# Forget attention: the causal mask added to the table on VectorE, and a pair's units from wide to narrow

## The chip, the cores and the metric

The kernel runs on one core of one Trainium2 chip. The metric is the device time of one execution in microseconds. TensorE multiplies, VectorE, ScalarE and GpSimd work on elements, SyncE and the other engines' queues start transfers. Each engine runs its own instruction stream in order, and waits on semaphores that the others raise.

## The reference, cut to what matters

The program is a whole two-block transformer on 512 tokens of width 1024. The change touches one operation of the second block, the causal softmax attention with forget gates: 8 heads of 64, blocks of 128 queries.

```python
def _forgetting_attention(q, k, v, log_f):
    c = jnp.cumsum(log_f, axis=1)
    ...
    def block(args):
        qi, ci, t0 = args
        s = jnp.einsum('bqhd,bkhd->bhqk', qi, k) * SCALE
        s = s + ci[..., None] - c_k[:, :, None, :]
        q_pos = t0 + jnp.arange(BLOCK_Q)
        s = jnp.where(k_pos[None, :] <= q_pos[:, None], s, NEG_INF_2)
        p = jax.nn.softmax(s, axis=-1)
        return jnp.einsum('bhqk,bkhd->bqhd', p.astype(v.dtype), v)
```

Ahead of it the same block computes a dilated attention of 8 more heads, which has a distance bias instead of the forget table. Behind it come the output projection, a router and the experts.

## The kernel before

Both attentions are computed by one loop over 32 units, listed in `TWO` (L1920): kind f (0 dilated, 1 forget), pair c of two heads, block i of 128 queries. A unit is as wide as its keys, (i + 1) x 128 columns (`width2`), so the four units of a pair go 128, 256, 384, 512. Units 0 to 15 are dilated, 16 to 31 forget. Every unit handles both heads of its pair (a = 0 and 1).

The steps of a unit:

- TensorE `scores(u)`: q times k of both heads into two PSUM banks, which alternate between units. In forget units two more products, `ident_b` times `causal_b` (L1989), add the mask (0 or -1e30, bf16) to the last 128 columns.
- VectorE `maxima(u)`: adds the table to the scores in PSUM and reduces the row's extreme (L2094), one instruction with an accumulator read for each head. For forget units the table is `CK[h]`, the head's forget sums, 512 columns wide in SBUF, the same for all four units of the pair.
- ScalarE `exps(u)`: exponentials and row sums (L2061).
- VectorE `normed(u)`: the reciprocal of the sums (L2099). It releases the scaling of the rows (L1960), which VectorE does for head 0 if the unit is wider than 256, and GpSimd for the rest, so for both heads of a narrow unit.
- TensorE `turned(u)`: transposes the rows in blocks (L1996). ScalarE copies head 0 out of PSUM (L2076), VectorE head 1 (L2119).
- TensorE `values(u)`: the rows times v (L2011), both heads, two products for each 128 keys.

The order is written out by hand. TensorE's iteration u is `scores(u + 2)`, `values(u - 1)`, `turned(u)`. VectorE's is `normed(u)`, `maxima(u + 2)`, after a pair's end `y2_low` (L2036, the low half of the finished output), and the copy of unit u. ScalarE's is `exps(u + 1)`, after a pair's end `y2_high` and `square2`, and its copy of unit u. GpSimd waits for each unit's reciprocal, scales, and after a pair adds up squares (L2132).

Three things are placed by unit number. `SUMS_AT = 22` puts the products that sum the dilated squares (L1965) ahead of the scores of unit 24, their result into `DIL_SUMS` (end of bank 0), its copy (L1970) ahead of that unit's maxima, and the split of a weight chunk of the output projection (L154, 128x2048, on VectorE) into iteration 24, behind the maxima of unit 26. `t_mx` is the semaphore that the maxima raise, 2 per unit, on which the exponentials wait, and SyncE too, for loading the second half of the forget table after unit 15.

Of the kernel before, what the change touches and what calls it, by code (L numbers as in the profile page):

```python
# [9 lines left out]
ALU = mybir.AluOpType  # L10
# [4 lines left out]
P = 128  # L15
D = 1024
T = 512
MT = T // P
# [44 lines left out]
def program(nc, a, out):  # L63
# [5 lines left out]
    with ctx:  # L69
# [37 lines left out]
        ident_b = sb("ident_b", [P, P], bf16)  # L107
# [1809 lines left out]
            src = bass.AP(bias_dram.tensor, half * 4 * TW, [[1, P], [TW, 4], [1, T]])  # L1917
            pool.dma_start(bias_raw[half], src).then_inc(b_ld, 16)

        TWO = [(f, c, i) for f in range(2) for c in range(4) for i in range(MT)]  # L1920
        NU2 = len(TWO)
        Y2_AT = {24: 0, 26: 1, 27: 2, 29: 3}
        tmin = sb("two_min", [P, 2, 2])
        tden = sb("two_den", [P, 4, 2])
        t_qk = Sig("attn_scores", NU2)
        t_mx = Sig("attn_max", 2 * NU2)
        t_ex = Sig("attn_exp", 2 * NU2)
        t_tr = Sig("attn_PT_mm", 2 * NU2)
        t_pa = Sig("attn_PT_head0", NU2)
# [14 lines left out]
        t_yl = Sig("attn_y_low", KT)  # L1944
        ACC = [JUNK[:, 0:512], WK[:, 0:512]]
        SQ = JUNK[:, 512:1024]
        SUMS_AT = 22

        def width2(u):
            return (TWO[u][2] + 1) * P  # L1950

        def normed2_at(u, a):
            wide = sum(width2(v) > 2 * P for v in range(u + 1))
# [15 lines left out]
            dve.wait_ge(t_ss, f + 1)  # L1969
            nc.vector.tensor_copy(stat[:, 8 + 4 * f:12 + 4 * f], o).then_inc(t_sc, 1)  # L1970

        DIL_SUMS, FOX_SUMS = PB[:, 0, 508:512], PB[:, 6, 0:4]

        def two_pe(pe):
            def scores(u):
                f, c, i = TWO[u]
                w = width2(u)
                q, k = ((qdT, kdT), (qfT, kfT))[f]
                if u >= 2:
                    pe.wait_ge(*t_ex.at(2 * u - 2))  # L1980
                if u == SUMS_AT + 2:
                    sums_pe(pe, 0, DIL_SUMS)
                for a in range(2):
                    h = slice(a * DH, (a + 1) * DH)
                    t = nc.tensor.matmul(PB[:, 2 * (u % 2) + a, 0:w], q[c][h, i * P:(i + 1) * P], k[c][h, 0:w],  # L1985
                                         start=True, stop=(f == 0))
                if f == 1:
                    for a in range(2):
                        t = nc.tensor.matmul(PB[:, 2 * (u % 2) + a, i * P:w], ident_b[:], causal_b[:], start=False, stop=True)  # L1989
                t.then_inc(t_qk.sem, 1)  # L1990

            def turned(u):
                for a in range(2):
                    pe.wait_ge(*normed2_at(u, a))
                    for b in range(width2(u) // P):
                        t = nc.tensor.transpose(PB[:, 4 + a, b * P:(b + 1) * P], PR2[:, u % 2, a, b * P:(b + 1) * P], ident[:])  # L1996
                    t.then_inc(t_tr.sem, 1)

            def values(u):
                f, c, i = TWO[u]  # L2000
                n = 4 * f + c
                if i == 0 and n >= 2:
                    pe.wait_ge(*t_yl.at(n - 1))
                    pe.wait_ge(*t_sq.at(n - 1))
                pe.wait_ge(*t_pa.at(u + 1))
                pe.wait_ge(*t_pb.at(u + 1))
                v0 = (VA_, VF_)[f] + c * P
                nb = width2(u) // P
                for b in range(nb):
                    for a in range(2):  # L2010
                        t = nc.tensor.matmul(PB[a * DH:(a + 1) * DH, 6 + n % 2, i * P:(i + 1) * P],  # L2011
                                             Z2[:, b, v0 + a * DH:v0 + (a + 1) * DH], PT2[u % 2][a][:, b, :],
                                             start=(b == 0), stop=(b == nb - 1))
                if i == MT - 1:
                    t.then_inc(t_out.sem, 1)

            p_2.wait_all(pe)
            turned_wait(pe, 4)
            scores(0)
            scores(1)  # L2020
            for u in range(NU2):
                if u + 2 < NU2:
                    scores(u + 2)
                if u >= 1:
                    values(u - 1)
                turned(u)
            values(NU2 - 1)
# [25 lines left out]

        def two_act(act):
            def exps(u):
                act.wait_ge(*t_mx.at(2 * u + 2))
                if u >= 2:
                    act.wait_ge(*t_tr.at(2 * u - 2))
                w = width2(u)
                for a in range(2):  # L2060
                    nc.scalar.activation(PR2[:, u % 2, a, 0:w], PB[:, 2 * (u % 2) + a, 0:w], ACT.Exp,  # L2061
                                         bias=tmin[:, u % 2, a:a + 1], scale=-1.0,
                                         accum_out=tden[:, u % 4, a:a + 1]).then_inc(t_ex.sem, 1)

            exps(0)
            for u in range(NU2):
# [8 lines left out]
                w = width2(u)  # L2075
# [7 lines left out]
        def two_dve(dve):  # L2083
            def maxima(u):
                f, c, i = TWO[u]
                w = width2(u)
                dve.wait_ge(*t_qk.at(u + 1))
                if u == SUMS_AT + 2:
                    sums_dve(dve, 0, DIL_SUMS)
                for a in range(2):  # L2090
                    h = 2 * c + a
                    table = CK[h][:, 0:w] if f else bias_raw[h // 4][:, h % 4, w - 1::-1]
                    s = PB[:, 2 * (u % 2) + a, 0:w]
                    nc.vector.tensor_tensor_reduce(s, s, table, -1.0, 3.0e38, ALU.add, ALU.min, tmin[:, u % 2, a:a + 1]  # L2094
                                                   ).then_inc(t_mx.sem, 1)
# [1104 lines left out]
```

## Time and profile before

| | |
|---|---|
| median of 3 runs | 1823.97 us (1823.07 to 1825.81) |
| the profiled execution's own time | 1824.19 us |
| its span in the profile | 1822.3 us |
| TensorE busy | 1769.0 us, 97% |
| VectorE busy | 866.0 us, 48% |
| ScalarE, GpSimd busy | 631.9 us (35%), 232.1 us (13%) |
| chain that ended last | TensorE 90%, VectorE 5%, ScalarE 3% |
| second attention stage | 1357 to 1440.6 us, forget half from about 1394 |

Times of the timeline count from the span's start. The profiled execution took 1.9 us more than its span. A row's duration is how long one instruction was in its engine; successive instructions of an engine overlap by some tens of ns up to 0.2 us, so the cost of one in a full stream is read from start to start.

### The profile page before, as it was taken

The numbers are of one execution on the slowest core, as the hardware profiler recorded it, in microseconds if no ns is written. First come the engines' busy times: TensorE is split into PE (matmuls) and PEld (weight loads), VectorE is DVE, ScalarE is ACT, GpSimd is POOL, SyncE is SP. The second block draws the span as 40 slices with busy tenths as digits, with TensorE's granted clock in tenths as the row PEclk, the third lists the DMA queues.
The fourth block names the chain that finished last, engine by engine and source line by source line (L and its number), as shares of the span: only waits on it lengthen the run. The fifth ranks groups of instructions, "written<-read, shape, count | busy, mean of one in ns | idle before, by whom it ended". The sixth has DMA issues, their size and how long they took to land.

```text
span 1822.3 us, 22718 instructions
## 1 busy us (share of the span) xinstructions
PE 1769.0 (97%) x9086; PEld 1301.2 (71%) x9086; DVE 866.0 (48%) x1684; ACT 631.9 (35%) x1257; POOL 232.1 (13%) x283
## 2 busy tenths in 40 slices
PE   7999999999999999999999999999999999999998
PEld 6778888888888887568888888888776674333333
DVE  4436544443366446745545443353447463333326
ACT  5236334332353224635443332253347430000002
POOL 4000000000000103310000000000004412333322
PEclk9999999999999998999999999999999999999999
DMA  7223333332232217403333322243230138999985
GB/s 242 92 71 85 101 92 92 92 106 102 93 121 93 70 63 228 117 24 93 93 92 98 107 96 93 93 138 93 71 115 24 56 156 350 369 377 395 392 348 184
DMA packets 182313, 260.41 MB, mean 143 GB/s; under 512 B 24785, under 2 KB 137633, under 8 KB 169936
## 3 DMA queue, kind: packets, MB, share of 16 engines
q1 hardware_dynamic: 159040, 204.66, 33.4%
q0 software_dynamic: 19152, 25.14, 4.5%
q10 hardware_dynamic: 4032, 29.36, 4.1%
q8 instruction: 63, 1.03, 0.2%
q14 instruction: 26, 0.21, 0.0%
HBM read 297.53 MB, written 27.82 MB: 179 GB/s over the span
## 4 chain that ended last, share of the span: by engine, by line
PE 90%; DVE 5%; ACT 3%; DMA 1%; issue 1%; POOL 0%; SPq 0%; DVEq 0%; ACTq 0%; POOLq 0%
PE PB L191 21%; PE PB L193 21%; PE PB L192 21%; PE PB L2762 9%; PE PB L2784 5%; PE PB L2751 1%; PE PB L1985 1%; PE PB L2011 1%; PE PB L1996 1%; PE PB L1589 1%; PE PB L1566 1%; DVE RING_R L154 1%; PE PB L322 1%; PE PB L1558 1%; ACT RING_R L169 1%
## 5 line engine op out<-in xcount | busy, mean ns | idle before, releaser
L191 PE MATMUL PB<-RING_R,OPS_R 128*128 128x512 f32 (+1 forms) x1056 | 414.5, 393 | 4.6 <-DVE RING_R L154 3.5
L193 PE MATMUL PB<-RING_R,OPS_R 128*128 128x512 f32 (+1 forms) x1056 | 409.0, 387 | 0.0
L192 PE MATMUL PB<-RING_R,OPS_R 128*128 128x512 f32 (+1 forms) x1056 | 408.8, 387 | 0.0
L171 DVE SCALAR_TENSOR_TENSOR RING_R<-RING,gains,RING_R 128x256 fp32r<-128x256 f32 (+2 forms) x456 | 219.4, 551 | 254.3 <-ACT RING_R L169 254.3
L191 PE MATMUL PB<-OPS_R,RING_R 128*128 128x512 f32 (+1 forms) x736 | 280.7, 381 | 0.0
L192 PE MATMUL PB<-OPS_R,RING_R 128*128 128x512 f32 (+1 forms) x736 | 279.5, 380 | 0.0
L193 PE MATMUL PB<-OPS_R,RING_R 128*128 128x512 f32 (+1 forms) x736 | 279.5, 380 | 0.0
L191 PEld LDWEIGHTS PB<-RING_R,OPS_R 128*128 128x128 f32 x1056 | 198.9, 188 | 48.0 <-DVE RING_R L154 4.7
L169 ACT ACTIVATE RING_R<-RING,gains 128x256 fp32r<-128x256 f32 (+2 forms) x456 | 209.9, 540 | 59.7 <-DMA RING<-in_w_in 48.1
L193 PEld LDWEIGHTS PB<-RING_R,OPS_R 128*128 128x128 f32 x1056 | 198.7, 188 | 40.5
L192 PEld LDWEIGHTS PB<-RING_R,OPS_R 128*128 128x128 f32 x1056 | 198.9, 188 | 38.7 <-issue 0.2
L154 DVE TENSOR_TENSOR RING_R<-RING,RING_R 128x2048 fp32r<-128x2048 f32 x40 | 91.6, 2293 | 185.8 <-ACT RING_R L151 185.7
L191 PEld LDWEIGHTS PB<-OPS_R,RING_R 128*128 128x128 f32 x736 | 138.4, 188 | 26.5 <-issue 0.5
L192 PEld LDWEIGHTS PB<-OPS_R,RING_R 128*128 128x128 f32 x736 | 138.4, 188 | 26.5 <-issue 0.5
L193 PEld LDWEIGHTS PB<-OPS_R,RING_R 128*128 128x128 f32 x736 | 138.4, 188 | 26.4
L151 ACT ACTIVATE RING_R<-RING 128x2048 fp32r<-128x2048 f32 x40 | 76.4, 1913 | 199.9 <-DMA RING<-in_ffn_w_down 137.0
L806 ACT ACTIVATE WK<-WK 128x512 f32<-128x512 f32 x44 | 27.8, 632 | 278.5 <-DVE WK L829 278.5
L2826 ACT ACTIVATE WK<-PB 128x256 f32<-128x256 f32 x24 | 9.2, 383 | 279.3 <-PE PB L2762 279.3
L2865 DVE TENSOR_TENSOR WK<-PB,WK 128x256 f32<-128x256 f32 x24 | 14.7, 614 | 142.1 <-ACT WK L2826 141.7
L399 ACT ACTIVATE Z<-PB,stat 128x512 f32<-128x512 f32 (+1 forms) x34 | 22.8, 674 | 113.8 <-PE PB L193 113.8
L829 DVE TENSOR_TENSOR WK<-PB,Y 128x512 f32<-128x512 f32 x44 | 30.4, 690 | 63.7 <-PE PB L193 63.2
L3011 POOL DMA_DIRECT2D GP<-in_od_cmp_v_w x1 | 1.2, 1173 | 460.6 <-DVE X L578 460.6
(395 smaller groups left out, 2061.4 us busy)
## 6 DMA issues: line engine op xcount, KB each, us to landing
RING<-in_ffn_w_gate SPq DMA_DIRECT2D x44, 512.0 KB, 4.0
RING<-in_ffn_w_up SPq DMA_DIRECT2D x44, 512.0 KB, 5.3
RING<-in_ffn_w_down SPq DMA_DIRECT2D x44, 512.0 KB, 4.0
RING<-in_w_expert_gate SPq DMA_DIRECT2D x16, 1024.0 KB
RING<-in_w_expert_up SPq DMA_DIRECT2D x16, 1024.0 KB
OPS<-in_w_expert_gate SPq DMA_DIRECT2D x16, 1024.0 KB
OPS<-in_w_expert_up SPq DMA_DIRECT2D x16, 1024.0 KB
Y<-in_w_expert_down ACTq DMA_DIRECT2D x14, 1024.0 KB
```

The lines of the kernel that those rows point to most:

```text
L151: nc.scalar.activation(RING_R[:, high], RING[:, raw], ACT.Copy).then_inc(s_whi, 1)
L154: nc.vector.tensor_tensor(RING_R[:, raw], RING[:, raw], RING_R[:, high].bitcast(fp32), ALU.subtract).then_inc(s_wlo, 1)
L169: t = nc.scalar.activation(high, raw, ACT.Copy, scale=g)
L171: t = nc.vector.scalar_tensor_tensor(by_k(RING_R, o)[:, :, k, :], raw, g, high.bitcast(fp32), ALU.mult, ALU.subtract)
L191: nc.tensor.matmul(o, x[0], w[0], start=start, stop=False)
L192: nc.tensor.matmul(o, x[0], w[1], start=False, stop=False)
L193: return nc.tensor.matmul(o, x[1], w[0], start=False, stop=stop)
L399: t = nc.scalar.activation(dst, src, func, scale=rstd) if self.norm.deferred else nc.scalar.activation(dst, src, func)
L806: nc.scalar.activation(SIL[:, k, :], SIL[:, k, :], ACT.Silu).then_inc(self.sl.sem, 1)
L829: nc.vector.tensor_tensor(SIL[:, k, :], PB[:, BANK[k], :], rows, ALU.mult).then_inc(self.gs.sem, 1)
L2762: t = nc.tensor.matmul(PB[h, 2 + s % 2, :], XgT[:, s % 2, k, h], moe_gu[g][:, b, :, k, :], start=(k == 0), stop=(k == KT - 1))
L2784: t = nc.tensor.matmul(PB[h, 6 + hf, :], HhT[:, s % 2, j, h], moe_d[s % 2][:, b, j, hf * 512:(hf + 1) * 512], start=(j == 0), stop=(j == 1))
```

## The change

TensorE's two mask products per forget unit go. In their place VectorE adds `causal_b` to the last 128 columns (`i * P` to `w`) of the head's table `CK[h]`, in place in SBUF, for both heads, before the maxima of the unit (L2095 of the new file), behind the wait for the unit's scores. Ahead of the additions it waits for its own maxima of the unit before, which read the same table; behind them it waits for the additions. Since a narrower unit does not read the columns that a wider one has masked, the forget units of a pair now run from 512 down to 128. The semaphore of the maxima counts four per forget unit. A pair's first and last unit are told by u % 4. `SUMS_AT` is 21, so that sums, their copy and the split stand one unit earlier, and `DIL_SUMS` lies in bank 2, whose unit (23) is 128 wide.

```diff
-        TWO = [(f, c, i) for f in range(2) for c in range(4) for i in range(MT)]
+        TWO = [(f, c, MT - 1 - i if f else i) for f in range(2) for c in range(4) for i in range(MT)]
...
-        t_mx = Sig("attn_max", 2 * NU2)
+        t_mx = Sig("attn_max", 3 * NU2)
...
-        SUMS_AT = 22
+        SUMS_AT = 21
...
+        def max_at(u, masked=0):
+            f = TWO[u][0]
+            return t_mx.at(2 * u + 2 * max(u - NU2 // 2, 0) + (masked or 2 + 2 * f))
...
-        DIL_SUMS, FOX_SUMS = PB[:, 0, 508:512], PB[:, 6, 0:4]
+        DIL_SUMS, FOX_SUMS = PB[:, 2, 508:512], PB[:, 6, 0:4]
...
-                                         start=True, stop=(f == 0))
-                if f == 1:
-                    for a in range(2):
-                        t = nc.tensor.matmul(PB[:, 2 * (u % 2) + a, i * P:w], ident_b[:], causal_b[:], start=False, stop=True)
+                                         start=True, stop=True)
...
-                if i == 0 and n >= 2:
+                if u % MT == 0 and n >= 2:
...
-                if i == MT - 1:
+                if u % MT == MT - 1:
...
-                act.wait_ge(*t_mx.at(2 * u + 2))
+                act.wait_ge(*max_at(u))
...
+                if f:
+                    dve.wait_ge(*max_at(u - 1))
+                    for a in range(2):
+                        last = CK[2 * c + a][:, i * P:w]
+                        nc.vector.tensor_tensor(last, last, causal_b[:], ALU.add).then_inc(t_mx.sem, 1)
+                    dve.wait_ge(*max_at(u, 2))
```

VectorE around a pair's end, before: from the copy of unit 17 to the first head of unit 20's maxima and on to the scaling of unit 19. COPY is L2119, TENSOR_SCALAR the scaling, ISA the maxima (PB is PSUM, Y holds the tables), SCALAR_TENSOR_TENSOR `y2_low`.

```order
L2119 COPY Z<-PB 128x256
L2099 RECIPROCAL two_den<-two_den 128x2
L1960 TENSOR_SCALAR ST<-ST,two_den,ones 128x384
L2094 ISA PB,two_min<-PB,Y 128x128
L2094 ISA two_min 128x1
L2094 ISA PB,two_min<-PB,Y 128x128
L2094 ISA two_min 128x1
L2036 SCALAR_TENSOR_TENSOR OPS_R<-PB,gains,OPS_R 128x512
L2119 COPY Z<-PB 128x384
L2099 RECIPROCAL two_den<-two_den 128x2
L1960 TENSOR_SCALAR ST<-ST,two_den,ones 128x512
```

The same place in the changed kernel, from the copy of unit 17 to the maxima of unit 20 and the reciprocal of unit 19:

```order
L2126 COPY Z<-PB 128x384
L2106 RECIPROCAL two_den<-two_den 128x2
L2095 TENSOR_TENSOR Y<-Y,causal_b 128x128 x2
L2101 ISA PB,two_min<-PB,Y 128x512
L2101 ISA two_min 128x1
L2101 ISA PB,two_min<-PB,Y 128x512
L2101 ISA two_min 128x1
L2037 SCALAR_TENSOR_TENSOR OPS_R<-PB,gains,OPS_R 128x512
L2126 COPY Z<-PB 128x256
L2106 RECIPROCAL two_den<-two_den 128x2
```

The two additions stand ahead of the maxima, the 512-wide maxima stand ahead of `y2_low` and of the copy of the 256-wide unit, and no scaling is VectorE's at a pair's end.

TensorE at the seam of the two attentions, before, from the scores of unit 16 (L1985), their masks (L1989), values (L2011) and turning (L1996) in turn:

```order
L1985 MATMUL PB<-Z 128x128 x2
L1989 MATMUL PB<-causal_b,ident_b 128x128 x2
L2011 MATMUL PB<-Z 64x128 x4
L1996 MATMUL PB<-ident,ST 128x128 x6
L1985 MATMUL PB<-Z 128x256 x2
L1989 MATMUL PB<-causal_b,ident_b 128x128 x2
L2011 MATMUL PB<-Z 64x128 x6
L1996 MATMUL PB<-ident,ST 128x128 x8
```

And in the changed kernel, from the scores of unit 16 on:

```order
L1989 MATMUL PB<-Z 128x512 x2
L2012 MATMUL PB<-Z 64x128 x4
L1997 MATMUL PB<-ident,ST 128x128 x6
L1989 MATMUL PB<-Z 128x384 x2
L2012 MATMUL PB<-Z 64x128 x6
L1997 MATMUL PB<-ident,ST 128x128 x8
L1989 MATMUL PB<-Z 128x256 x2
L2012 MATMUL PB<-Z 64x128 x8
```

The mask products are gone, and the wide scores come first, so that unit 16 is as wide as unit 15.

## Rows read from the trace of the kernel before

**Rows 1.** The page: engine, busy us (share of the span), instructions

```profile
PE 1769.0 (97%) x9086; PEld 1301.2 (71%) x9086; DVE 866.0 (48%) x1684; ACT 631.9 (35%) x1257; POOL 232.1 (13%) x283
```

**Rows 2.** Chain that ended last, forget half: start us, us, engine, tile, line

```profile
1394.52 0.81 PE PB L2011 x12
...
1404.30 0.81 PE PB L2011 x12
...
1408.59 1.06 PE PB L1985 x4
1409.65 0.22 PE PB L1989 x2
...
1410.23 0.59 PE PB L1996 x4
...
1414.49 0.81 PE PB L2011 x12
...
1427.11 0.81 PE PB L2011 x12
...
1440.64 0.43 PE PB L191
```

**Rows 3.** Timeline of VectorE, one pair: start us, us, line, operation, idle before

```profile
1401.39 0.42 DVE L2119 COPY Z<-PB 128x256 f32<-128x256 f32 x1
1401.72 0.16 DVE L2099 RECIPROCAL two_den<-two_den 128x2 f32<-128x2 f32 x1
1401.92 0.48 DVE L1960 TENSOR_SCALAR ST<-ST,two_den,ones 128x384 f32<-128x384 f32 x1
1402.31 0.29 DVE L2094 CUSTOM_DVE_ANT_0 PB<-PB,Y 128x128 f32<-128x128 f32 x1
...
1402.77 0.75 DVE L2036 SCALAR_TENSOR_TENSOR OPS_R<-PB,gains,OPS_R 128x512 fp32r<-128x512 f32 x1
1403.49 0.56 DVE L2119 COPY Z<-PB 128x384 f32<-128x384 f32 x1
1403.96 0.15 DVE L2099 RECIPROCAL two_den<-two_den 128x2 f32<-128x2 f32 x1
1404.15 0.55 DVE L1960 TENSOR_SCALAR ST<-ST,two_den,ones 128x512 f32<-128x512 f32 x1
1404.62 0.42 DVE L2094 CUSTOM_DVE_ANT_0 PB<-PB,Y 128x256 f32<-128x256 f32 x1
...
1406.17 0.69 DVE L2119 COPY Z<-PB 128x512 f32<-128x512 f32 x1 [0.69 <-PE PB L1996]
...
1407.23 0.57 DVE L2094 CUSTOM_DVE_ANT_0 PB<-PB,Y 128x384 f32<-128x384 f32 x1 [0.30 <-PE PB L1989]
...
1408.63 0.29 DVE L2119 COPY Z<-PB 128x128 f32<-128x128 f32 x1 [0.25 <-PE PB L1996]
...
1409.90 0.70 DVE L2094 CUSTOM_DVE_ANT_0 PB<-PB,Y 128x512 f32<-128x512 f32 x1 [0.91 <-PE PB L1989]
```

**Rows 4.** TensorE behind the split, and busy time by stretch with granted clock (PEclk)

```profile
1421.06 0.44 PE L2011 MATMUL PB<-Z 128*64 128x128 f32 x4 [1.00 <-DVE Z L2119]
...
1423.00:1427.00 4.00, 4.00 (x24) 2.50 (x22) 2.97 (x11) 2.50 (x9) 2.61 (x3) 0.57 0.00 0
```

**Rows 5.** Groups by line and shape, VectorE: busy us, mean ns, idle before

```profile
L2427 DVE TENSOR_TENSOR Z<-Z 128x128 f32<-128x128 f32 x4 | 1.2, 292 | 0.1
```

**Rows 6.** Timelines of VectorE and GpSimd in an earlier stage

```profile
573.20 6.09 DVE L171 SCALAR_TENSOR_TENSOR RING_R<-RING,gains,RING_R 128x512 fp32r<-128x512 f32 x4
...
573.37 4.05 POOL L1177 TENSOR_TENSOR Z<-Z,gam 128x2048 f32<-128x2048 f32 x1 [46.06 <-DVE Z L1167]
...
583.35 2.74 DVE L171 SCALAR_TENSOR_TENSOR RING_R<-RING,gains,RING_R 128x512 fp32r<-128x512 f32 x4 [3.40 <-ACT RING_R L169]
```

**Rows 7.** Timeline of GpSimd in the forget half: scaling of a 512-wide unit

```profile
1404.22 1.03 POOL L1960 TENSOR_SCALAR ST<-ST,two_den,ones 128x512 f32<-128x512 f32 x1
```

**Rows 8.** Timeline of TensorE at the end of the attention

```profile
1439.55 1.09 PE L2011 MATMUL PB<-Z 128*64 128x128 f32 x16 [0.88 <-DVE Z L2119]
```

## The prediction, made before the changed kernel ran

> **What bounds the kernel now.** I read the page first, then the chain of waits through the second attention stage, then the timelines of the engines in it. TensorE is busy for 97% of the span [rows 1], so whatever delays its stream delays the end. The change lies in the forget half of the attention, units 16 to 31, some 47 of 1822 us. The chain passes through the value products of every fourth unit [rows 2]: units 14, 18, 22 and 26 start at 1394.52, 1404.30, 1414.49 and 1427.11, and the first product of the output projection follows at 1440.64. The steps are 9.78, 10.19, 12.62 and 13.53 us, and these four are what the change has to beat. The plain pair takes 9.78 us.
>
> In that pair VectorE idles 0.69, 0.30, 0.25 and 0.91 us [rows 3], 2.15 in all: it works 7.6 us and TensorE nearly all of 9.8. It is the second busiest engine, and each unit's second head must pass through its copy (L2119) before TensorE can use it. The page's 48% for VectorE over the whole span hides this.
>
> The third step holds two things that are not the pair's. VectorE splits a weight chunk in 2.2 us (L154), and TensorE waits 1.00 us for the copy behind it; then its mean granted clock is 0.57 over 4 us [rows 4], mostly at its lower level of 1.2 GHz. Work lost there: 4 x 0.43 = 1.7 us.
>
> **What goes.** 32 mask products on TensorE, two per unit at 0.22 us the two [rows 2]: 16 x 0.22 = 3.5 us. That is the most that their going can give, and only if TensorE stays the engine that is waited for.
>
> **What comes.** 32 additions on VectorE, 128x128 each, both operands in SBUF. Before has none in this place; the nearest row is an addition of the same size elsewhere, 0.29 us [rows 5]. Successive instructions overlap: a 128-wide maximum of 0.29 us lets its accumulator read start 0.21 later (the two heads take 0.46, 1402.31 to 1402.77), so I take 0.20 for the first of two and 0.29 for the second. The maxima wait until both are written; the reciprocal, 0.16 long, lets what waits for it start 0.20 after its own start [rows 3], so 0.04 to 0.06 more. Together 0.55 us a unit, 8.8 us in all. At the least, with the second fully overlapped, 0.40; at the most, two full durations and the wait, 0.65.
> Where they stand matters more than their sum. They come after the wait for the unit's scores, so none of them can run while VectorE waits for scores. Queued behind them are the maxima, which the exponentials need, and the copy of the unit two before, which TensorE's value products need.
> The extra wait for the unit before costs nothing: those maxima were issued several instructions earlier.
>
> **The port, the term that I weigh most.** At 573.37 GpSimd runs a product of two SBUF tensors for 4.05 us. VectorE is then in a group of four instructions that also read two SBUF tensors each; the group takes 6.09 us, and the same group takes 2.74 at 583.35 [rows 6]. The 3.35 us more is what was left of GpSimd's instruction. So such a VectorE instruction waits until GpSimd is done. The maxima (one operand in PSUM) do not show this, but the added instructions have both operands in SBUF. They also come at the worst moment: the reciprocal releases GpSimd, which starts scaling 0.26 us after the reciprocal's start (1403.96, 1404.22) and takes 1.03 us for a 512-wide unit [rows 3, 7], so it ends 1.29 after. VectorE reaches the addition 0.19 + 0.47 = 0.66 after [rows 3]. Wait: 0.6 us for a 512-wide unit, by the same reckoning 0.5 for a 384-wide one, and for the narrow ones 0.2 and 0, since one is held back by its scores until GpSimd is in its first of two scalings and the other is issued before GpSimd starts. Per pair 1.3 us.
> The Trainium skill's page "SBUF — State Buffer", section "SBUF: two separate sides", says that a VectorE instruction with two SBUF inputs and a GpSimd instruction that reads SBUF take one shared pair of ports in turn, whichever is first for its whole length. By it each addition would wait as above; if only VectorE's two-results modes locked the ports, it would not. The rows at 573 us agree with the rule.
>
> **A pair after the change, on VectorE.** Start to start [rows 3]: copies 0.34 + 0.20 + 0.61 + 0.48 = 1.6; reciprocals and the wide scalings 0.08 + 0.08 + 0.66 + 0.59 = 1.4; maxima 0.46 + 0.72 + 1.00 + 1.27 = 3.45; the low half 0.72; together 7.2. Additions 4 x 0.55 = 2.2. Port 1.3. One wait remains: before the next pair's first maxima the scores, 512 wide, take 1.06 us from the end of the turning [rows 2], while VectorE has 0.56 to do, so 0.5. Sum 11.2 us against 9.78. VectorE becomes the bound, and the mask products taken from TensorE buy nothing more. The four steps:
> - Up to unit 14: its copy stands behind unit 16's additions (0.55), their port wait (0.5) and 512-wide maxima in place of 128-wide ones (1.27 for 0.46). It had hardly any slack: +1.85.
> - Unit 14 to 18: here two 512-wide units stand side by side, since the last dilated unit is wide as well. Copies 2.2, reciprocals and scalings 2.0, maxima 3.45, low half 0.7, additions 2.2, port 0.6 + 0.6 + 0.5 + 0.2 = 1.9, wait 0.5, less 0.1 as the last copy is the shorter: 12.8 against 9.78, +3.0.
> - Unit 18 to 22: 11.2 against 10.19, +1.0. The sums of squares on TensorE (moved a unit earlier, other bank) now lie beside VectorE's work.
> - Unit 22 to 26: 11.2 + 2.2 for the split, no longer covered by any idle time, 13.4 against 12.62: +0.8. To this I add the clock. TensorE will wait some 2 us behind the split, longer than the 1.0 before, so I take the 1.7 us again, +2.5.
> - Unit 26 to the end: 5.0 on VectorE to the values of unit 28, then TensorE and the copies by turns. The last four units go 512 to 128 instead of 128 to 512, so 20 value products at 0.81 for 6 [rows 2] are 2.8 with little beside them, turns at 0.59 for 4 are 1.8 for 12, waits for GpSimd 0.5, copies 0.7 + 0.6 + 0.45. Sum 11.9 against 13.53, -1.6. The last wait is for a copy of 128 columns, not of 512 as at 1439.55 [rows 8].
> Sum: 1.85 + 3.0 + 1.0 + 2.5 - 1.6 = +6.75. What follows is TensorE's own stream, so nothing takes it back. The profiled execution took 1824.19 us, 0.22 over the median of 1823.97: 1830.9 by the one, **1830.7** on the median's footing.
>
> **Rivals.**
> - No port conflict: the additions cost 0.55 and no more. For it: no row shows GpSimd's scaling itself holding up VectorE, and the additions may slip in before it. Against it: [rows 6]. Without the port waits a pair is 10.6 (the wait for scores grows, the bound passes partly back) and the walk gives +3.0: 1827.0.
> - More half-speed clock: TensorE's idle time in the half rises from 4 to over 14 us, most of it at the seam, behind the split and at the end. Two stretches more as in [rows 4], 1.7 each: 1834. Against it: where VectorE is the bound, a slower TensorE is partly hidden, and the wait of 0.88 near the end [rows 8] was followed by no fall.
> - Not slower: VectorE's 2.15 us of idle time takes the 2.2 us of additions in. Then the seam costs the wide maxima, 0.8; a pair keeps TensorE's time without masks, 3 x -0.35; the split +1.0; the end -1.6. Sum -0.9: 1823.1, or 1821.4 without the half-speed stretch. It decides at whether an addition with its wait costs under some 0.1 us beyond what VectorE waits at that unit. Against it: 0.91 of the 2.15 is a wait for scores, which the additions stand behind, and the order puts the wide maxima ahead of the narrow unit's copy.
>
> **How the numbers follow.** Forecast 0.58, no port 0.22, more half speed 0.10, not slower 0.10. The range holds the additions at 0.40 (-2.4) and 0.65, the port from nothing to full, and one half-speed stretch more or less: 1825.2 to 1834.3, leaving out most of the last case and the far end of the third. A measurement of this kernel tells 0.2%, 3.6 us, from no change; over 1827.6 is slower. The forecast and the third case lie there, with a part of the second: 0.72. Within 0.2%: 0.24. Faster: 0.04.
>
> **What would show it.** Right: the additions take 0.29 us or, beside GpSimd's scaling, 0.7 to 0.9; VectorE idle under 1 us per plain pair; value products 11.2 us apart from unit 18 to 22; TensorE waiting for L2119's copy (another line number there) about 1 us per pair and some 2 us behind the split. Wrong: additions all at 0.3 us or under (then the second case), the pair at 9.5 us (then the last), granted clock under 1 in more than 4 us (then the third). I would also be wrong if the work after the attention did not simply shift.

## The result and the profile after

| | before | after |
|---|---|---|
| median, us | 1823.93 (1823.07 to 1825.81, 6 runs) | 1830.25 (1829.21 to 1834.88, 6 runs) |
| profiled execution, us | 1824.19 | 1832.51 |
| its span, us | 1822.3 | 1830.6 |

The changed kernel is slower: ratio 1.0038, 95% interval 1.0025 to 1.0051, some 6.3 us by the medians (forecast 6.7) and 8.3 us between the two profiled spans.

The page of after, engine, busy us (share of the span), instructions, to be read against [rows 1]:

```profile
PE 1770.3 (97%) x9054; PEld 1301.1 (71%) x9054; DVE 876.6 (48%) x1716; ACT 633.5 (35%) x1257; POOL 233.9 (13%) x283
```

TensorE has 32 instructions fewer, VectorE 32 more and 10.6 us more work. TensorE's busy time did not fall, although 3.5 us of mask products are gone: this profiled execution holds about as much more time at the lower clock, as is seen below. Now the value products of after, from TensorE's timeline (start us, us, line, shape, idle time before and what ended it), and as the last row the first product of the output projection. They answer to [rows 2] and [rows 4]:

```profile
1392.44 0.44 PE L2012 MATMUL PB<-Z 128*64 128x128 f32 x4
...
1398.20 0.88 PE L2012 MATMUL PB<-Z 128*64 128x128 f32 x12 [1.35 <-DVE Z L2126]
...
1410.47 0.66 PE L2012 MATMUL PB<-Z 128*64 128x128 f32 x8 [0.84 <-DVE Z L2126]
...
1421.51 0.66 PE L2012 MATMUL PB<-Z 128*64 128x128 f32 x8 [0.84 <-DVE Z L2126]
...
1425.49 0.70 PE L2012 MATMUL PB<-Z 128*64 128x128 f32 x4 [1.91 <-DVE Z L2126]
...
1435.05 0.66 PE L2012 MATMUL PB<-Z 128*64 128x128 f32 x8 [0.84 <-DVE Z L2126]
...
1446.98 0.50 PE L191 MATMUL PB<-RING_R,OPS_R 128*128 128x512 f32 x1
```

Units 12, 14, 18, 22 and 26 are the rows at 1392.44, 1398.20, 1410.47, 1421.51 and 1435.05; the row at 1425.49 is unit 23, behind the split. In before's timeline unit 12's and unit 14's products and the first of the output projection stand at:

```profile
1390.23 0.44 PE L2011 MATMUL PB<-Z 128*64 128x128 f32 x4
...
1394.45 0.88 PE L2011 MATMUL PB<-Z 128*64 128x128 f32 x12
...
1440.57 0.50 PE L191 MATMUL PB<-RING_R,OPS_R 128*128 128x512 f32 x1
```

The chain of [rows 2] dates the same products 0.07 us later (1394.52, 1440.64), so only its differences are used. This gives where the 8.3 us are, in us:

| stretch | before | after | difference | forecast |
|---|---|---|---|---|
| up to unit 12, untouched by the change | 1390.23 | 1392.44 | +2.2 | 0 |
| unit 12 to 14, the seam | 4.22 | 5.76 | +1.5 | +1.85 |
| 14 to 18 | 9.78 | 12.27 | +2.5 | +3.0 |
| 18 to 22 | 10.19 | 11.04 | +0.9 | +1.0 |
| 22 to 26 | 12.62 | 13.54 | +0.9 | +2.5 |
| 26 to the output projection | 13.53 | 11.93 | -1.6 | -1.6 |
| behind it, to the end of the span | 381.7 | 383.6 | +1.9 | 0 |

The change's own part is the five rows in the middle: +4.2 us. The first and the last row are stretches in which no instruction changed. The table of stretches (us, busy time and instructions of TensorE, its weight loads, VectorE, ScalarE and GpSimd, then the granted clock, share and GB/s of the DMA), of before and then of after, shows what differs there:

```profile
1357.00:1395.00 38.00, 34.71 (x290) 20.86 (x292) 29.70 (x111) 28.23 (x91) 17.47 (x26) 1.00 0.21 74
1510.00:1518.00 8.00, 7.72 (x44) 5.21 (x45) 3.37 (x12) 0.00 (x0) 3.14 (x4) 0.79 0.96 386
```
```profile
1357.00:1393.00 36.00, 32.22 (x254) 18.44 (x252) 25.40 (x96) 25.13 (x80) 14.75 (x23) 0.95 0.17 59
1425.00:1429.00 4.00, 3.36 (x18) 2.46 (x19) 3.49 (x13) 1.41 (x4) 1.17 (x2) 0.57 0.00 0
1514.00:1526.00 12.00, 9.96 (x48) 6.71 (x46) 5.58 (x18) 0.00 (x0) 3.92 (x4) 0.72 0.92 366
```

Ahead of unit 12 the mean granted clock is 0.95 in after against 1.00. Behind the attention the part below full speed costs 12 x 0.28 = 3.4 us in after and 8 x 0.21 = 1.7 in before. So this profiled execution holds some 3.5 us more of the lower level, 1.2 GHz, in stretches of unchanged work. The first of these cannot come from the change: the granted clock was below 1 between 1360 and 1366 us (0.60 and 0.83 over 3 us each), and the first changed instructions, the scores of unit 16, start at 1393.47.

One pair of the forget half on VectorE, after (start us, us, line, idle before), which answers to [rows 3], and GpSimd beside it, which answers to [rows 7]:

```profile
1404.34 0.48 DVE L1964 TENSOR_SCALAR ST<-ST,two_den,ones 128x384 f32<-128x384 f32 x1
1404.74 0.79 DVE L2095 TENSOR_TENSOR Y<-Y,causal_b 128x128 f32<-128x128 f32 x2
...
1407.39 0.56 DVE L2095 TENSOR_TENSOR Y<-Y,causal_b 128x128 f32<-128x128 f32 x2 [0.44 <-PE PB L1989]
...
1410.31 0.47 DVE L2095 TENSOR_TENSOR Y<-Y,causal_b 128x128 f32<-128x128 f32 x2
...
1412.35 0.55 DVE L1964 TENSOR_SCALAR ST<-ST,two_den,ones 128x512 f32<-128x512 f32 x1
1412.81 0.90 DVE L2095 TENSOR_TENSOR Y<-Y,causal_b 128x128 f32<-128x128 f32 x2
```
```profile
1404.41 0.99 POOL L1964 TENSOR_SCALAR ST<-ST,two_den,ones 128x384 f32<-128x384 f32 x1 [1.84 <-DVE two_den L2106]
...
1412.41 1.17 POOL L1964 TENSOR_SCALAR ST<-ST,two_den,ones 128x512 f32<-128x512 f32 x1 [0.88 <-DVE two_den L2106]
```

The one wait of VectorE that these rows mark is the 0.44 us for scores; in before it had 2.15 us of idle time per pair. The two additions of a unit take 0.47 to 0.56 us where GpSimd is idle or narrow, and 0.79 and 0.90 where its wide scaling runs. GpSimd's own 512-wide scaling grew from 1.03 to 1.17 us: both engines pay. TensorE now waits 0.84 us per plain pair and 1.91 us behind the split, all for VectorE's copy.

### The profile page after: what moved, and what is told of

Its sections match the earlier page's. It is cut to its first block, busy times and chain, and to the rows that moved or that the text cites. A ratio compares the mean times of both kernels' runs of the same rounds, so it can differ in the third digit from the quotient of the medians.

```text
span 1830.6 us, 22700 instructions
## 1 busy us (share of the span) xinstructions
PE 1770.3 (97%) x9054; PEld 1301.1 (71%) x9054; DVE 876.6 (48%) x1716; ACT 633.5 (35%) x1257; POOL 233.9 (13%) x283
## 3 DMA queue, kind: packets, MB, share of 16 engines
q8 instruction: 63, 1.03, 0.2%
## 4 chain that ended last, share of the span: by engine, by line
PE 89%; DVE 6%; ACT 3%; issue 1%; DMA 1%; POOL 0%; SPq 0%; DVEq 0%; POOLq 0%
PE PB L191 21%; PE PB L193 21%; PE PB L192 21%; PE PB L2769 9%; PE PB L2791 5%; PE PB L2758 1%; PE PB L1589 1%; PE PB L1566 1%; PE PB L1989 1%; PE PB L1997 1%; DVE RING_R L154 1%; PE PB L1558 1%; DVE PB L2101 1%; PE PB L2012 1%; PE PB L322 1%
## 6 DMA issues: line engine op xcount, KB each, us to landing
RING<-in_w_expert_up SPq DMA_DIRECT2D x16, 1024.0 KB, 11.7
```

## The experiments

Ratios are to the kernel before, timed beside it, with 95% intervals; 0.1% is 1.8 us. The steps are those of the table above, read off TensorE's timeline of each profiled execution, in us. A star marks a step with more than 2 us at the lower clock in it.

| kernel | ratio | 12 to 14 | 14 to 18 | 18 to 22 | 22 to 26 | 26 on | sum |
|---|---|---|---|---|---|---|---|
| before | 1 | 4.22 | 9.78 | 10.19 | 12.62* | 13.53 | 50.3 |
| after, run again | 1.0037 (1.0023 to 1.0051) | 5.75 | 12.26 | 11.04 | 13.53* | 11.92 | 54.5 |
| e1 order only | 1.0014 (1.0006 to 1.0023) | 5.13 | 11.47 | 10.70 | 11.84 | 11.49 | 50.6 |
| e2 order, no mask | 1.0007 (0.9998 to 1.0015) | 4.93 | 11.26 | 10.29 | 13.98* | 11.49 | 52.0 |
| e3 both masks | 1.0057 (1.0045 to 1.0069) | 6.90 | 12.42 | 11.71 | 14.22* | 12.13 | 57.4 |
| e4 late additions | 1.0037 (1.0024 to 1.0049) | 5.32 | 11.63 | 11.01 | 15.05* | 12.30 | 55.3 |
| e5 after, GpSimd small | 1.0016 (1.0007 to 1.0025) | 5.45 | 11.78 | 10.68 | 13.69* | 10.93 | 52.5 |
| e6 before, GpSimd small | 0.9997 (0.9988 to 1.0006) | 4.19 | 9.74 | 10.19 | 10.66 | 13.50 | 48.3 |
| e7 additions doubled | 1.0066 (1.0042 to 1.0089) | 7.24 | 13.72 | 13.11* | 15.16* | 12.71 | 61.9 |
| e8 additions on GpSimd | 1.0033 (1.0020 to 1.0046) | 5.47 | 11.90 | 11.27 | 12.86* | 12.76 | 54.3 |
| e9 before, no mask | 0.9984 (0.9971 to 0.9998) | 4.19 | 9.41 | 9.66 | 10.88 | 13.21 | 47.4 |
| e10 before, split in four | 0.9997 (0.9981 to 1.0013) | 4.22 | 9.77 | 10.19 | 9.77 | 13.53 | 47.5 |
| e11 e8, two waits moved | 1.0058 (1.0036 to 1.0079) | 5.47 | 12.00 | 13.44* | 10.32 | 14.58* | 55.8 |

**After, run again.** The changed kernel beside the experiments, as their footing.

> The changed kernel once more, unedited, on the chip of the next three: 1830.3, 6.3 us over before. Its second profile shows how much of the first one's 8.3 us more span lies outside the forget half: my theory says the forget half takes 48 to 49 us again, and what lies outside it differs by 1 to 3 us with the stretches of half clock alone.

The forget half comes out the same to 0.02 us per step. What differs between its profiled executions lies outside. Unit 12 starts at 1392.42 again, but the clock is at full speed from 1354 us up to there: here the time was lost earlier, at a mean granted clock of 0.81 from 690 to 720 us and 0.96 to 750, where before has 0.83 and 1.00.

### The change taken apart

**e1, the order alone.** Units of a pair from wide to narrow, the mask still by TensorE's products. The sums and the split stand one unit earlier, as in after.

```diff
-        TWO = [(f, c, i) for f in range(2) for c in range(4) for i in range(MT)]
+        TWO = [(f, c, MT - 1 - i if f else i) for f in range(2) for c in range(4) for i in range(MT)]
```

> The changed kernel with TensorE's mask products back and VectorE's additions left out: of the change only the order from wide to narrow and what hangs on it. My theory (VectorE is the bound only because of the additions): the seam costs the wide maxima, the split is exposed more, the end is shorter; 1.1 us slower than before, 1825.0; value products of units 14, 18, 22, 26 about 11.4, 10.5, 11.7 us apart plus what half clock adds. Rival (the order itself is what costs): 4 us or more slower than before.

**e2, after without the additions.** The causal mask isn't computed.

```diff
-                    for a in range(2):
-                        last = CK[2 * c + a][:, i * P:w]
-                        nc.vector.tensor_tensor(last, last, causal_b[:], ALU.add).then_inc(t_mx.sem, 1)
```

> The changed kernel with the additions left out and no mask at all (the causal mask of the forget attention is missing, so this part of the computation is not done). My theory: this minus the changed kernel is the price of the additions with their port waits; 0.3 us faster than before, 1823.6, and 6 to 7 us faster than the changed kernel's 1830.3. Against the order-only kernel the mask products are worth 1.4 us. Rival (additions are cheap, something else made the changed kernel slow): 1828 or more.

**e3, additions and mask products together.**

```diff
+                if f == 1:
+                    for a in range(2):
+                        t = nc.tensor.matmul(PB[:, 2 * (u % 2) + a, i * P:w], ident_b[:], causal_b[:], start=False, stop=True)
```

> The changed kernel with TensorE's mask products kept beside the additions. My theory (VectorE is the bound, with one wait for scores a pair): the products cost about 0.3 us a pair through the wait for the wide scores, 1.0 us in all, 1831.3. Rival (TensorE still bounds the pair): 16 x 0.22 = 3.5 us, 1833.8.

**e9, before without its mask products.** The causal mask isn't computed.

```diff
-                if f == 1:
-                    for a in range(2):
-                        t = nc.tensor.matmul(PB[:, 2 * (u % 2) + a, i * P:w], ident_b[:], causal_b[:], start=False, stop=True)
```

> The kernel before without its 32 mask products, and without any mask: the causal mask of the forget half is not computed. It gives the most that taking the products off TensorE can bring, whatever replaces them. Theory: TensorE waits for VectorE in the forget half, so that of 32 x 0.22/2 = 3.5 us of mask products (pairs of 0.22 us) most only lengthens those waits; 1 to 2 us less, 1822 to 1823 us. Rival (TensorE's stream sets the half): 3.5 us less, 1820.5 us.

Together they give a ledger by the medians: the order +0.14% (2.6 us), the products' going -0.07% (1.3 us, from e1 to e2), the additions +0.30% (5.5 us, from e2 to after). Each of these has an interval of its own: the order's runs from 1.1 to 4.2 us, the additions', as the difference of two measured ratios, from some 2.5 to 8.5, and the intervals of e1 and e2 overlap, so that the products' going is not established in this order. The steps are sharper, where no lower clock lies in them. From e2 to after the four steps other than the third are 3.0 us longer. From e1 to after, which puts the additions in place of the products, all five are 3.9 longer, of which after's half-speed stretch is some 0.4, and the medians say 0.23%, 4.2 us. That VectorE's additions cost more than TensorE's products did is thus shown twice.

e9 gives 0.16% (2.9 us) for the products in the old order, of which its third step holds 1.7, and those are the half-speed stretch that it doesn't have. Its first two steps are 0.37 and 0.53 us shorter, for 0.9 us of products taken out of each. So products are paid for at about half, as TensorE partly waits anyway.

e3's extra products cost 2.9 us on after by the sum of the steps and 3.6 by the medians, with intervals that overlap a little; both lie nearer to the rival's 3.5 than to my 1.0. But it is not TensorE's own time that the trace shows there. VectorE's wait for scores grows from 0.44 to 0.65 us in the plain pair (1405.22), as my theory had it. And 1.15 us of the 2.9 lie in the seam, where the additions come later and so meet GpSimd's sum of squares. VectorE and GpSimd of e3 at the seam:

```profile
1391.40 1.78 DVE L2098 TENSOR_TENSOR Y<-Y,causal_b 128x128 f32<-128x128 f32 x2
```
```profile
1390.90 0.87 POOL L1964 TENSOR_SCALAR ST<-ST,two_den,ones 128x384 f32<-128x384 f32 x1 [1.37 <-DVE two_den L2109]
1391.73 1.30 POOL L2142 TENSOR_TENSOR WK<-WK 128x512 f32<-128x512 f32 x1
```

The two additions take 1.78 us in place of after's 0.80 at this point and end 0.15 us after GpSimd does (1393.03). So a delay of 0.3 us turned into one of a whole GpSimd instruction.

The order's +2.6 us are not in e1's steps as they stand: they sum to 50.6 against 50.3. The seam and the first two steps are 0.9, 1.7 and 0.5 us longer than before's without any addition in them, the third and the last 0.8 and 2.0 shorter. But before's third step has a half-speed stretch that e1's hasn't, 1.96 us by e6 below; with that set aside the order costs 2.2, near the medians' figure. My walk of the steps (11.4, 10.5, 11.7) was right to 0.2 us each. That the wide unit's maxima, ahead of the copies for which TensorE waits, are what costs is my reading of the order and wasn't tried by itself.

### Where the additions' time comes from

**e7, twice the additions.** The second result goes to a buffer that nobody reads.

```diff
+                        nc.vector.tensor_tensor(STG[:, 2 * P * a:2 * P * a + P], last, causal_b[:], ALU.add)
                         nc.vector.tensor_tensor(last, last, causal_b[:], ALU.add).then_inc(t_mx.sem, 1)
```

> The changed kernel with a second addition per head, whose result goes to a buffer nobody reads: 32 additions more, two per unit of the forget half. Theory (VectorE sets the pair of the forget half, so that each of its instructions is paid in full): 16 units by 2 x 0.27 us (the shortest addition of the changed kernel's trace) is 8.7 us over the changed kernel, somewhat more where a second addition also meets GpSimd's scaling and somewhat less at the seam with the other half; 1838 to 1840 us. Additions' groups per unit in the trace: four of about 0.27 to 0.3, or 0.7 for the one beside the scaling. Rival (the additions sit mostly in VectorE's idle time and the time comes from the order, the waits and the clock): under 3 us over the changed kernel, 1831 to 1834 us.

1837.24 us median, 0.29% (5.3 us) over after, in the middle between the two figures, with an interval that reaches from under 1 to 10 us. The steps tell more. From unit 18 to 22, where no seam and no split lies, the step grew by 13.11 - 11.04 = 2.07 us for eight additions: 0.26 each, the whole of an addition's length. All five steps together grew by 7.4 us for 8.7 us of additions, the seam by 1.5, the step after it by 1.5, the last by 0.8. VectorE is the bound in a plain pair; over the whole half a VectorE microsecond costs 0.85 by the steps and 0.6 by the medians.

**e5 and e6, GpSimd's scaling cut to one column**, in after and in before. The rows it should scale stay unscaled.

```diff
-            p = PR2[:, u % 2, a, 0:width2(u)]
+            p = PR2[:, u % 2, a, 0:1 if eng is nc.gpsimd else width2(u)]
```

> The changed kernel with GpSimd scaling one column of each row block in place of all (the rows of those heads stay unscaled, so that part of the computation is left out). GpSimd then holds its ports for next to nothing. Port theory: all pairs of additions take 0.5 us, where the changed kernel has 0.8 and 0.9 in wide units; a pair 10.6 us instead of 11.0, the forget half 3 us shorter, 1827. Rival (the long additions have another cause, such as the table's own columns): they stay at 0.8 to 0.9 and the time at 1830.

> The kernel before with the same one-column scaling on GpSimd (same part left out): the control for what GpSimd's scaling costs without the additions. Walk: 0.5 us faster than before. If it gains as much as the same edit gains on the changed kernel, the port wait is no part of the change's price.

The same edit takes 0.21% (3.8 us) off after and 0.03% (0.5 us) off before. The addition beside the scaling of a 512-wide unit, in VectorE's timeline of e5 and in the same columns as above, lost its extra time (0.90 in after):

```profile
1408.91 0.49 DVE L2095 TENSOR_TENSOR Y<-Y,causal_b 128x128 f32<-128x128 f32 x2
```

So the collision is real. By the medians some 3 us of the additions' 5.5 are owed to it; by the steps e5 is 2.0 us shorter than after, 1.1 in the seam and the first two steps and 1.0 in the last, where the scaled rows themselves are also ready earlier. e6 rules that out as a gain only for the old order (0.1 us in its four steps without the split), so 2 to 3 us is the most that these runs give the collision. e7 shows how it goes, because there each addition stands alone. Its VectorE and GpSimd at two 512-wide units:

```profile
1416.01 0.61 DVE L2095 TENSOR_TENSOR STG<-Y,causal_b 128x128 f32<-128x128 f32 x1
1416.54 0.28 DVE L2096 TENSOR_TENSOR Y<-Y,causal_b 128x128 f32<-128x128 f32 x1
...
1431.15 0.28 DVE L2095 TENSOR_TENSOR STG<-Y,causal_b 128x128 f32<-128x128 f32 x1
1431.36 0.70 DVE L2096 TENSOR_TENSOR Y<-Y,causal_b 128x128 f32<-128x128 f32 x1
```
```profile
1415.44 1.04 POOL L1964 TENSOR_SCALAR ST<-ST,two_den,ones 128x512 f32<-128x512 f32 x1 [0.90 <-DVE two_den L2107]
...
1430.76 1.16 POOL L1964 TENSOR_SCALAR ST<-ST,two_den,ones 128x512 f32<-128x512 f32 x1 [3.10 <-DVE two_den L2107]
```

At 1416.01 the addition is held until GpSimd is done (1416.48) and ends 0.14 us later. At 1431.15 one addition runs at its usual 0.28 in the middle of GpSimd's instruction, which takes 1.16 in place of 1.04; the next is held, and ends 0.14 us after GpSimd's end at 1431.92. The Trainium skill's page "SBUF — State Buffer", section "SBUF: two separate sides", has it that whoever is first keeps the shared ports for its whole instruction. The held additions agree. The one that got through at 1431.15 does not, if GpSimd holds the ports from its instruction's recorded start. In e7 it started 0.39 us into GpSimd's instruction, and the held one at 1416.01 started 0.57 us in. In after the pairs of additions that start 0.33 to 0.40 us into a wide scaling lengthen it by 0.11 to 0.14 us in the same way, but for one, at 1415.74, which starts 0.40 in. So GpSimd may take the ports only some 0.4 us after its recorded start; the traces don't show when it does.

**e4, the additions late,** for the unit three later, behind the copy, where GpSimd is idle.

```diff
                 nc.vector.tensor_copy(PT2[u % 2][1][:, 0:w // P, :].rearrange("p k n -> p (k n)"), PB[:, 5, 0:w]).then_inc(t_pb.sem, 1)
+                if NU2 // 2 <= u + 3 < NU2:
+                    masked(u + 3)
```

> The changed kernel with each unit's additions moved ahead: issued right behind VectorE's copy of the unit three before, when GpSimd has mostly done its scaling, and no longer behind the wait for the unit's scores. Same instructions. My theory (half of the additions' price is the port wait and the place): additions at 0.3 us nearly all, 3 us slower than before, 1827.0, so 3 to 4 us faster than the changed kernel. Rival (the price is the additions' own time): 1829.5 to 1830.5, as the changed kernel.

1830.8 us, as slow as after: my forecast of this run was wrong. The collision did go. VectorE's timeline of e4, then TensorE's:

```profile
1409.96 0.48 DVE L2107 TENSOR_TENSOR Y<-Y,causal_b 128x128 f32<-128x128 f32 x2
1410.37 0.16 DVE L2111 RECIPROCAL two_den<-two_den 128x2 f32<-128x2 f32 x1
1410.56 0.55 DVE L1964 TENSOR_SCALAR ST<-ST,two_den,ones 128x512 f32<-128x512 f32 x1
```
```profile
1408.96 0.76 PE L1997 MATMUL PB<-ident,ST 128*128 128x128 f32 x2 [0.28 <-POOL ST L1964]
...
1411.16 1.21 PE L1997 MATMUL PB<-ident,ST 128*128 128x128 f32 x8 [0.44 <-DVE ST L1964]
```

The additions now stand ahead of the reciprocal and delay it, and both scalings behind it, by 0.4 us. TensorE waits for the scaled rows (0.28 and 0.44) in place of the copy, and the plain pair is again 11.0. The seam and the first step did gain, 0.4 and 0.6 us; the last lost 0.4, and a longer half-speed stretch behind the split, 0.57 over 8 us (15.05 in the third step), took a further 1.5. In the plain pair a wait was swapped for another of the same size.

**e8, the additions on GpSimd,** for the unit three later, behind its scaling.

```diff
+                    for a in range(2):
+                        last = CK[2 * TWO[v][1] + a][:, TWO[v][2] * P:width2(v)]
+                        nc.gpsimd.tensor_tensor(last, last, causal_b[:], ALU.add).then_inc(t_mx.sem, 1)
```

> The changed kernel with the same additions made by GpSimd, for the unit three later, behind its own scaling of the unit. Theory (only VectorE's time counts, and GpSimd has about 7 us idle per pair): VectorE loses 0.55 us per unit, but the additions on GpSimd, which no trace of these kernels shows at this width (its 128x512 scaling takes 1.03 us, so 0.3 to 0.6 us each is an estimate), lie beside VectorE's minima and turn-copies and lengthen some of them; 1827 to 1830 us. Rival (what costs is any addition into the table, since it meets the other engine at the port wherever it is made): 1831 us or more, with minima of 128x512 over the 0.65 us that they take in the changed kernel.

1830.06 us median, just over the first figure's upper end, and 0.0004 under after, which can't be told from it. The minima are not lengthened (0.715 us at 512 columns, 0.716 in after), so the second figure's reason is wrong. GpSimd's timeline of e8, then TensorE's:

```profile
1406.26 0.81 POOL L2149 TENSOR_TENSOR Y<-Y,causal_b 128x128 f32<-128x128 f32 x2 [0.73 <-DVE two_min L2097]
1407.03 1.27 POOL L2135 TENSOR_TENSOR WK<-WK 128x512 f32<-128x512 f32 x1
1408.28 0.88 POOL L1964 TENSOR_SCALAR ST<-ST,two_den,ones 128x128 f32<-128x128 f32 x2
```
```profile
1408.79 0.76 PE L1997 MATMUL PB<-ident,ST 128*128 128x128 f32 x2 [0.87 <-POOL ST L1964]
```

The reciprocal for the scaling at 1408.28 had started at 1407.03. GpSimd's additions pushed its sum of squares in front of it, and TensorE stood 0.87 us: idle time on GpSimd was there on average, not where it was needed.

**e11, e8 with the squares behind the next scaling and VectorE's split in four parts.**

```diff
-                if u >= 6 and u % 4 == 2:
+                if u >= 7 and u % 4 == 3:
                     added(u // 4 - 1)
```

The split's edit is that of e10, below: four parts of 512 columns, one in each pair, and ScalarE's part of the split in unit 11.

> The additions on GpSimd as in the run before it, with two waits taken out: GpSimd adds the squares (1.27 us) behind the 128-wide unit's scaling instead of ahead of it, and VectorE's split of the weight chunk is cut into four parts of 512 columns, one per pair. Theory (what is left of the in-place mask's cost are TensorE's waits, 0.87 us for the scaling behind the squares in each of three pairs, and 2.2 us for the split): the steps are 10.9, 10.4, 10.4 and 12.4 in place of 11.90, 11.27, 12.86 and 12.76, so 4 to 5 us less than the run before it, 1825 to 1827 us, the same as the kernel before. Rival (GpSimd and VectorE collide at the port whatever the order, now also in the parts of the split): no part of a split under 0.9 us where GpSimd works, the steps lose under 2 us, 1828 us or more.

1834.29 us: the first figure was off by 8. GpSimd's timeline of e11, TensorE's, and the table of stretches:

```profile
1409.89 1.13 POOL L2161 TENSOR_TENSOR Y<-Y,causal_b 128x128 f32<-128x128 f32 x2 [0.27 <-DVE two_min L2109]
1410.98 1.45 POOL L2147 TENSOR_TENSOR WK<-WK 128x512 f32<-128x512 f32 x1
1412.42 0.77 POOL L1964 TENSOR_SCALAR ST<-ST,two_den,ones 128x512 f32<-128x512 f32 x1
```
```profile
1413.24 0.66 PE L1997 MATMUL PB<-ident,ST 128*128 128x128 f32 x4 [1.22 <-POOL ST L1964]
```
```profile
1414.00:1418.00 4.00, 4.00 (x31) 3.43 (x31) 1.85 (x8) 2.08 (x6) 1.68 (x3) 0.57 0.01 2
```

Beside the split's part (1409.66 to 1410.35) GpSimd's additions took 1.13 us for 0.81, and the squares, now ahead of the 512-wide scaling, 1.45 for 1.27. The wait of 0.87 became one of 1.22, and the granted clock fell behind it. In the last step the same came again, a wait of 1.23 at 1437.00 and a clock of 0.59 and 0.56 from 1438 to 1442. Only the third step did what I had expected, 10.32 for 12.86.

**e10, before with VectorE's split in four.**

```diff
-                if u == SUMS_AT + 2:
-                    split_to(dve, "dve", d_2.n0 + 3)
+                if u in (15, 19, 23, 27):
+                    split_part(u // 4 - 3)
```

> The kernel before with VectorE's 2.2 us split of the weight chunk cut in four of 512 columns, placed in units 15, 19, 23 and 27, where VectorE idles 0.65 to 0.7 us before its 512-wide copy, and ScalarE's part of it moved to unit 11. If the split's uncovered wait (1.2 us) and the half-speed clock behind it (1.7 us) go: 2 to 3 us faster than before, 1822. Rival (the half-speed stretch comes somewhere else then, or the pieces delay the copies): no difference.

In before the same cut takes the third step from 12.62 to 9.77, a plain pair, and the clock stays at full speed there. The time is nonetheless the same, 0.9997, with runs from 1821.9 to 1830.8. The profiled execution has its half-speed stretch elsewhere, in the half ahead:

```profile
1357.00:1366.00 9.00, 7.55 (x32) 3.36 (x32) 4.90 (x22) 5.71 (x17) 2.01 (x5) 0.62 0.65 233
1416.00:1430.00 14.00, 13.73 (x132) 8.75 (x128) 11.84 (x41) 8.98 (x31) 7.02 (x10) 1.00 0.01 1
```

That is 9 x 0.38 = 3.4 us lost for 2.85 won. The cut can't have caused it: the stretch ends by 1366, and the first instruction that this kernel has elsewhere, ScalarE's part of the split, starts at 1387.05. So the profiled execution doesn't show that the half-speed stretch moved because of the cut, and the 2.85 us are within the interval of the medians. Apart from e9, which leaves out the mask, none of these kernels is shown to beat before.

## Why the prediction came out right, and which terms did not

- **VectorE becomes the bound.** Right. One marked wait of 0.44 us in a pair (0.5 forecast), TensorE waits 0.84 per pair (1 forecast) and 1.91 behind the split (2 forecast). e7's 2.07 us for eight additions from unit 18 to 22 shows it apart from the reckoning.
- **The additions, 0.55 a unit.** Right: 0.47 to 0.56 free of GpSimd, 0.47 to 0.49 in e5.
- **The port, 1.3 us a pair.** Right in kind, too large. Against e5's lengths the wait is 0.41 at 512 columns and 0.31 at 384, not 0.6 and 0.5: one of the two additions can slip into GpSimd's instruction, and the held one ends 0.14 us after it, not a full length. That is 0.5 us less in each pair. It shows in the first step, +2.5 for +3.0, and at the seam, +1.5 for +1.85. In the second step it is mostly taken back, +0.85 for +1.0: VectorE idles 0.17 and 0.50 us there where I had one wait of 0.5, and copies the sums.
- **The mask products buy nothing more.** Nearly: e1 and e2 give 1.3 us for them, not established. e3 shows the other way in which a product costs: it delays the additions into a longer GpSimd instruction.
- **The end, -1.6.** Right, -1.6.
- **The clock behind the split, +1.7 in full.** This step failed. The stretch came (0.57 over 4 us from 1425), but after's step was 13.54 for a forecast of 13.4 without it. In these 4 us VectorE was busy for 3.49, and in the whole step it waited for the slow TensorE once:

```profile
1428.13 0.69 DVE L2126 COPY Z<-PB 128x512 f32<-128x512 f32 x1 [0.40 <-PE PB L1997]
```

The copies of a 512-wide unit at 1403.54, 1414.48 and 1439.07 have no such wait. So of the 1.7 us some 0.4 were paid, and the rest was hidden behind the engine that is the bound. Before paid for it, as e6 shows: without the stretch its third step is 10.66 in place of 12.62. The term should have been 13.4 - 12.62 = +0.8, and +0.9 was measured: the 0.5 us too much for the port and the 0.4 of the clock nearly cancel. The prediction names this hiding, but under the rival of more half-speed clock, and not in its own sum.

- **What follows simply shifts.** Wrong for the profiled execution: 1.9 us behind the attention and 2.2 ahead of unit 12 came on top, both with a lower granted clock.

So the forecast of 6.7 us held for 6.3, but not by its own sum, and in part by luck. The forget half gave 4.2; the two terms that were too large, 1.6 for the clock and 0.8 for the port in the first step and the seam, were made up elsewhere. The rival of two more half-speed stretches came true in this execution's clock, but in stretches of unchanged work, and not where it had put them.

Whether the change causes any of that isn't shown, and the other kernels speak for chance. In the 14 profiled executions unit 12 starts between 1388.9 (e3) and 1392.4 us (after), with e10 at 1392.2, and what lies behind the attention takes from 381.3 (e11) to 384.0 (after, run again), with e9, a kernel without any addition, at 383.3. Before stands at 1390.2 and 381.7 in these ranges, so 4 us of difference outside the half lies within what unchanged work scatters. The medians lean the other way: the half's 4.2 us are 0.23%, at or just under the lower ends of the two intervals of after, 0.25% and 0.23%, so a part of what came on top may be the change's.

## What to carry to other kernels

A step taken off the busiest engine is worth what that engine doesn't wait for anyway, and the same step put on the engine that it waits for is paid nearly in full (0.26 us of 0.28 per addition in a plain pair here); the list of waits in one pair tells this, the share of busy time over the span doesn't. Before an instruction with two SBUF operands is put on VectorE, look at what GpSimd does at that very moment, and before work goes to an idle engine, at whom it stands in front of. When a half-speed stretch is seen in the profile, ask which engine is the bound in it before its loss is added to a sum. And before a difference between two profiles is put down to a change, look at stretches that lie ahead of its first instruction: here they differ by up to 3.5 us.

## What the runs showed of the hardware that I had not expected

- A wait of TensorE does not by its length alone bring the clock down. Behind the split it waited 1.00 us in before, and the granted clock fell to 0.57; it waited the same 1.00 us in e6, 1.13 in e9 and 1.36 in e1, and the clock stayed at full speed. At e7's seam it stayed there behind 2.83 us. e6, e1 and e7, TensorE's timeline and the stretch of each:

```profile
1420.99 0.44 PE L2011 MATMUL PB<-Z 128*64 128x128 f32 x4 [1.00 <-DVE Z L2119]
```
```profile
1416.00:1430.00 14.00, 13.00 (x115) 7.70 (x113) 11.86 (x36) 9.43 (x31) 4.48 (x10) 1.00 0.01 1
```
```profile
1421.43 0.44 PE L2015 MATMUL PB<-Z 128*64 128x128 f32 x4 [1.36 <-DVE Z L2123]
```
```profile
1416.00:1430.00 14.00, 12.00 (x100) 7.11 (x100) 11.72 (x36) 9.53 (x28) 5.29 (x8) 1.00 0.01 1
```
```profile
1399.52 0.88 PE L2012 MATMUL PB<-Z 128*64 128x128 f32 x12 [2.83 <-DVE Z L2127]
```
```profile
1395.00:1414.00 19.00, 12.84 (x118) 8.33 (x116) 18.36 (x59) 9.89 (x29) 8.18 (x9) 1.00 0.17 56
```

- A stretch of 0.57 over 4 us costs about 1.7 us where TensorE is the bound (12.62 against 10.66 leaves 1.96, with the rest of e6's edit) and cost some 0.4 where VectorE was, so which of them an execution catches moves a profile by more than most terms of this case.
- GpSimd's addition of 128x128 takes 0.43 us (median of 32 in e8) against VectorE's 0.28, and VectorE's 512-column subtraction beside it stretches two of them from 0.81 to 1.13. The collision works in this direction too with a long instruction: in e8 two of them stand 2.73 us beside VectorE's split of 2.29:

```profile
1419.70 2.73 POOL L2149 TENSOR_TENSOR Y<-Y,causal_b 128x128 f32<-128x128 f32 x2 [0.27 <-DVE two_min L2097]
```
```profile
1419.48 2.29 DVE L154 TENSOR_TENSOR RING_R<-RING,RING_R 128x2048 fp32r<-128x2048 f32 x1
```
